# Result stores of an expert stage moved from SyncE's to ScalarE's DMA queue, tokens picked from the residual, and a ninth weight slot

## The reference

```python
def expert_block(args):
    tok_b, e = args
    xb = xpad[tok_b]
    h = jax.nn.silu(xb @ w_gate[e]) * (xb @ w_up[e])
    return h @ w_down[e]
...
out = out.reshape(rows, d) * buf_wt[:, None].astype(out.dtype)
y = jnp.zeros((t + 1, d), out.dtype).at[buf_tok].add(out)[:t]
```

## Time and profile before

| | |
|---|---|
| median of 3 runs | 1660.17 us (1656.58 to 1660.31) |
| profiled execution, its own time | 1661.11 us |
| its span | 1659.4 us |
| TensorE matmul busy | 1412.8 us (85%) |
| VectorE, ScalarE busy | 682.1 us (41%), 479.2 us (29%) |
| moved by DMA | 339.26 MB, mean 204 GB/s |
| expert stage | from about 290 to 864 us of the span |

### The profile page before, as it was taken

How to read it: one execution, slowest core, us unless ns; L and a number is a source line. 1 busy time by engine, 2 the same in 40 slices (tenths; PEclk the granted TensorE clock), 3 DMA queues, 4 the chain that set the end, 5 groups by cost and what they waited for, 6 DMA issues and landing times.

```text
span 1659.4 us, 24134 instructions
## 1 busy us (share of the span) xinstructions
PE 1412.8 (85%) x9624; PEld 1060.5 (64%) x9624; DVE 682.1 (41%) x1238; ACT 479.2 (29%) x753; POOL 40.2 (2%) x79
## 2 busy tenths in 40 slices
PE   6999997878866767796544999997999999999976
PEld 5786776645544443364223888875888888888865
DVE  4576745110111001010006656445436666656645
ACT  5452431000000000000015222233334444444432
POOL 2000000000000000000011100000000000000000
PEclk9998997989988899999876999997999999999988
DMA  8937324898999973399956555210221212121101
GB/s 351 398 127 279 127 102 203 326 406 361 380 379 423 383 327 152 139 410 395 422 224 247 214 203 182 109 52 27 102 102 51 102 52 102 52 102 52 51 1 64
DMA packets 38375, 339.26 MB, mean 204 GB/s; under 512 B 3784, under 2 KB 9800, under 8 KB 19400
## 3 DMA queue, kind: packets, MB, share of 16 engines
q1 hardware_dynamic: 30584, 302.33, 45.7%
q0 software_dynamic: 7200, 34.08, 5.8%
q10 hardware_dynamic: 432, 0.60, 0.1%
HBM read 312.62 MB, written 24.38 MB: 203 GB/s over the span
## 4 chain that ended last, share of the span: by engine, by line
PE 42%; DMA 4%; DVE 3%; ACT 2%; SPq 1%; issue 1%; POOL 0%; DVEq 0%; ACTq 0%; PEldq 0%; POOLq 0%
PE ps L285 41%; DMA y_scratch<-ar 4%; PE ps L732 1%; SPq L2087 1%; ACT ar L882 0%; DVE b_NL L1326 0%; DMA ar<-y_scratch,rt 0%; DVE ar L1318 0%; DVE hres L1796 0%; DVE hres L1789 0%; ACT b_NH L891 0%; DVE ar L1979 0%; ACT ar L1110 0%; ACT ar L1106 0%; DVE ar L1277 0%
## 5 line engine op out<-in xcount | busy, mean ns | idle before, releaser
L285 PE MATMUL ps<-ar 128*32 128x256 f32 (+5 forms) x1486 | 267.4, 397 | 53.7 <-ACT ar L1026 20.8
L285 PEld LDWEIGHTS ps<-ar 128*128 128x128 f32 (+3 forms) x1486 | 178.2, 163 | 128.5 <-issue 91.4
L285 PE MATMUL ps<-ring,ar 128*32 128x256 f32 (+1 forms) x2272 | 200.8, 411 | 47.6 <-DMA ring<-in_wts_dram 15.1
L285 PE MATMUL ps<-b_NH,b_WH 128*128 128x512 f32 x704 | 187.1, 401 | 9.5 <-ACT b_NH L891 5.1
L285 PE MATMUL ps<-b_NH,b_WL 128*128 128x512 f32 x704 | 181.0, 393 | 0.0
L1259 DVE TENSOR_TENSOR b_WL<-ring,b_WH 128x1024 fp32r<-128x1024 f32 x112 | 136.5, 1220 | 99.7 <-ACT b_WH L834 99.7
L285 PEld LDWEIGHTS ps<-ring,ar 128*32 128x32 f32 (+1 forms) x2272 | 105.4, 117 | 109.8 <-issue 61.3
L285 PE MATMUL ps<-b_NL,b_WH 128*128 128x512 f32 x704 | 173.7, 389 | 0.0
L285 PE MATMUL ps<-spare,ar 128*32 128x256 f32 (+1 forms) x1680 | 138.6, 415 | 39.4 <-ACT ar L1023 13.2
L834 ACT ACTIVATE b_WH<-ring 128x1024 fp32r<-128x1024 f32 x112 | 118.1, 1055 | 162.8 <-PE ps L285 159.8
L1689 DVE TENSOR_TENSOR ar<-ar,ps 128x128 f32<-128x128 f32 x46 | 13.1, 287 | 361.9 <-ACT ar L1020 358.6
(11 more groups left out here) (267 smaller groups left out, 1655.5 us busy)
## 6 DMA issues: line engine op xcount, KB each, us to landing
ring<-in_wts_dram SPq DMA_DIRECT2D x84, 2048.0 KB, 16.2
spare<-in_wts_dram SPq DMA_DIRECT2D x36, 2048.0 KB, 21.1
ar<-in_wts_dram SPq DMA_DIRECT2D x12, 2048.0 KB, 18.7
y_scratch<-gate POOLq DMA_DIRECT2D x15, 1024.0 KB, 25.5
ring<-in_wmod_dram SPq DMA_DIRECT2D x24, 512.0 KB, 4.6
ar<-in_wmod_dram POOLq DMA_DIRECT2D x24, 512.0 KB, 4.3
y_scratch<-ar SPq DMA_DIRECT2D x50, 128.0 KB, 2.3
hres<-in_x_dram SPq DMA_DIRECT2D x4, 512.0 KB, 6.8
```

The lines of the kernel that those rows point to most:

```text
L285: return pe.matmul(o, l, m, start=start, stop=stop, skip_group_check=True)
```

## The change

It has five parts:

- The y stores, of main, second and third blocks, are issued by ScalarE on its own queue, right behind the copy that they store. ScalarE waits for its own copy's semaphore before it issues. In the branches without a second or third block it now also waits for the landing counters `oy` and `ty` and raises them. SyncE keeps the loads; for a third block it waits for the last matmul (`t_d2`) in place of the copy.
- The picks read the residual `hres` itself; VectorE multiplies the pick matrix with the norm's factor `rs`, four more products for each set (and four in a third block).
- The first 16 KB of `ar` in each partition, where xs was, become a ninth slot, used once TensorE has transposed xs.
- The loads run nine panels ahead, so a load of expert n + 3 takes the place of the same panel of expert n.
- `mod_columns` and `mod_gate` (products for the second block's modulation) both stand behind the matmuls that rank the tokens.

```diff
-        slots = [ring[:, j, :] for j in range(RING)] + [area(4096, 4096)] + [spare[:, j, :] for j in range(3)]
+        slots = [ring[:, j, :] for j in range(RING)] + [area(4096, 4096), area(0, 4096)] + [spare[:, j, :] for j in range(3)]
...
-        for i, j in enumerate((2, 4, 0, 1, 5, 6, 7, 3)):
+        for i, j in enumerate((2, 4, 0, 1, 5, 6, 7, 8, 3)):
             settle(P_MOE + i, j)
...
-                        t = mm(ps[:, b, (k % 2) * 256:(k % 2) * 256 + 256], xs[:, p, k * 128:(k + 1) * 128],
+                        t = mm(ps[:, b, (k % 2) * 256:(k % 2) * 256 + 256], hres[:, p, k * 128:(k + 1) * 128],
                                OH[:, p, :], p == 0, p == 3)
...
+            def store(n, s):
+
+                return act.dma_start(y_d[n * CAP:(n + 1) * CAP, :].rearrange("t (q c) -> q t c", q=4), ysb[s])
...
                 copy_y(s, 5).then_inc(S["m_y"], 1)
+                act.wait_ge(S["m_y"], n + 1)
+                store(n, s).then_inc(S[f"y{s}"], 16)
...
                     copy_y(2, 7).then_inc(S["o_y"], 1)
+                    act.wait_ge(S["o_y"], n + 1)
+                    store(NE + n, 2).then_inc(S["oy"], 16)
                 with act.Else():
                     if n:
                         act.wait_ge(S["o_ht"], n)
                         act.wait_ge(S["o_y"], n)
+                        act.wait_ge(S["oy"], 16 * n)
                     act.sem_inc(S["o_ht"], 1)
                     act.sem_inc(S["o_y"], 1)
+                    act.sem_inc(S["oy"], 16)
...
+                for p in range(4):
+                    dve.wait_ge(S["m_e"], n_e[0] + 6 + p)
+                    t = dve.tensor_scalar(o[:, p, :], o[:, p, :], rs[:, p:p + 1], None, ALU.mult)
...
+            sp.wait_ge(S["turn"], 16)
+            load(P_MOE + 4)
             sp.wait_ge(S["rt_pe"], 1)
-            for i in range(P_MOE + 4, P_MOE + 7):
+            for i in range(P_MOE + 5, P_MOE + 8):
                 load(i)
...
                 with sp.If(third(n)):
-                    sp.wait_ge(S["t_y"], n + 1)
...
+                    sp.wait_ge(S["t_d2"], n + 1)
                 for m in range(3):
-                    i = P_MOE + 3 * n + m + 8
+                    i = P_MOE + 3 * n + m + 9
                     if i < P_C0:
                         load(i)
...
-                sp.wait_ge(S["m_y"], n + 1)
-                store(n, n % 2).then_inc(S[f"y{n % 2}"], 16)
```

More of the change, by code:

```diff
@@ L69, in program @@
         s_un = [ctx.enter_context(nc.semaphore(f"s_un{p}")) for p in range(4)]
-        s_slot = [ctx.enter_context(nc.semaphore(f"s_slot{j}")) for j in range(8)]
+        s_slot = [ctx.enter_context(nc.semaphore(f"s_slot{j}")) for j in range(9)]
         s_yg = [ctx.enter_context(nc.semaphore(f"s_yg{m}")) for m in range(8)]
@@ L136, in program @@
             settle(i, j)
-        for i, j in enumerate((2, 4, 0, 1, 5, 6, 7, 3)):
+        for i, j in enumerate((2, 4, 0, 1, 5, 6, 7, 8, 3)):
             settle(P_MOE + i, j)
-        for i in range(P_MOE + 8, P_C0):
-            settle(i, place[i - 8])
-        free_ring = [place[p] for p in range(P_C0 - 8, P_C0) if place[p] < RING]
+        for i in range(P_MOE + 9, P_C0):
+            settle(i, place[i - 9])
+        free_ring = [place[p] for p in range(P_C0 - 9, P_C0) if place[p] < RING]
         for i in range(P_C0, P_DIL):
@@ L517, in tensor_program @@
             t.then_inc(S["rt_pe"], 1)
+            pe.wait_ge(S["md"], 24)
+            mod_columns(acc0)
             mod_gate(acc0, (1, 6))
@@ L1026, in copy_y, with store_third @@
                 return act.activation(ysb[s], ps[:, b, 0:256], ACT.Copy)
+            def store(n, s):
+                return act.dma_start(y_d[n * CAP:(n + 1) * CAP, :].rearrange("t (q c) -> q t c", q=4), ysb[s])
+            def store_third(u):
+                r = 2 * NE * CAP + WIDE * u
+                for hf in range(2):
+                    act.dma_start(y_d[r:r + WIDE, hf * 512:(hf + 1) * 512],
+                                 ysb3[64 * hf:64 * hf + 64, :]).then_inc(S["ty"], 16)
             def third_block(u):
@@ L1039, in third_block @@
                 act.activation(ysb3, ps[:, 7, :], ACT.Copy).then_inc(S["t_y"], 1)
+                act.wait_ge(S["t_y"], u + 1)
+                store_third(u)
             act.wait_ge(S["ctl"], 1)
@@ L1724, in third_block @@
                 for p in range(4):
-                    dve.wait_ge(S["t_e"], 5 * u + 2 + p)
-                    t = dve.scalar_tensor_tensor(out=OH3[:, p, :], in0=i256[:, 0:64], scalar=rel[:, 4 + p:5 + p],
-                                                 in1=OH3[:, p, :], op0=ALU.is_equal, op1=ALU.add)
+                    dve.wait_ge(S["t_e"], 9 * u + 2 + p)
+                    dve.scalar_tensor_tensor(out=OH3[:, p, :], in0=i256[:, 0:64], scalar=rel[:, 4 + p:5 + p],
+                                             in1=OH3[:, p, :], op0=ALU.is_equal, op1=ALU.add).then_inc(S["t_e"], 1)
+                for p in range(4):
+                    dve.wait_ge(S["t_e"], 9 * u + 6 + p)
+                    t = dve.tensor_scalar(OH3[:, p, :], OH3[:, p, :], rs[:, p:p + 1], None, ALU.mult)
                 t.then_inc(S["t_oh"], 1)
@@ L2139, in sync_program @@
                         load(P_C0)
-                sp.wait_ge(S["m_y"], n + 1)
-                store(n, n % 2).then_inc(S[f"y{n % 2}"], 16)
-                with sp.If(second(n)):
-                    sp.wait_ge(S["o_y"], n + 1)
-                    if n:
-                        sp.wait_ge(S["oy"], 16 * n)
-                    store(NE + n, 2).then_inc(S["oy"], 16)
-                with sp.Else():
-                    if n:
-                        sp.wait_ge(S["oy"], 16 * n)
-                    sp.sem_inc(S["oy"], 16)
             for j in range(NOV):
```

42 lines of the change are left out of this document (13 added, 29 removed).

## The result

The changed kernel takes 1688.89 us (median of 4 runs, 1681.94 to 1692.62), the kernel before 1659.93 us in the runs beside it: a ratio of 1.0174, 95% interval 1.0137 to 1.0212, so 29 us slower. The profiled execution took 1686.87 us, 1685.1 us of it the span.

A forecast was written before the change was run, and what follows sets the result against it. Four DMA engines carrying all stores besides their weight share bound the expert stage. Terms 37.5 - 4.9 - 3.4 + 1.1 = +30 us on the median 1660.17 gave 1690 us, leaned to 1691; range 1663 to 1716.

The forecast's parts named there:

- What bounds: Expert stage: four DMA engines carry all stores besides their weight share; 510 us of work in 565 us.
- In this order the wait costs little: Expert stage before: ScalarE's 132.6 us of store waits cost little, since the four engines are working meanwhile.
- Stores on ScalarE's queue: Expert stage: queues alternate packet for packet, so a store takes 21 us while weights are queued; +37.5 us, bounds +12 to +55.
- Four dry spells: Engines idle after experts 1, 8, 15 and 22, for 6.5, 6.3, 2.6 and 5.1 us: +20.5 us.
- Issue on ScalarE: ScalarE's 46 store issues take 15 to 23 us, already in the sum; being held in issues 0, bound 0 to 10 us.
- Hole: Third blocks of experts 19 and 20: SyncE waits for the last matmul instead, one more panel in hand; -3.4 us.
- Ninth slot: Weight loads: one panel more before the loop, one less in it, on the four engines; -4.9 us.
- Factor in the pick matrix: Before the first pick: four more VectorE products, +1.1 us; the other sets lie beside TensorE's up, 0.
- Gate's matmuls later: Ahead of the picks: columns and gate end inside the wait for the pick matrix; 0, or up to +2 us.
- The store isn't held up: Rival, expert stage: small store packets go together or ahead, ScalarE's waits vanish; -26 us, 1634 us; 13%.
- Worse: Rival: ScalarE held in its issues and TensorE's lower clock at each dry spell; 1718 us at most, 1712 likely; 12%.
- the recurrence: "Latest of what it waits for" through all 32 experts; for the kernel before, expert 31's copy at 855 us, trace 858.8.

The follow-up runs named there:

- b_scalar_stores: Kernel before with only its y stores moved to ScalarE's queue, with the waits that go with them; 1689.5 us, ratio 1.0196.
- a_16_engines: Changed kernel with each y store issued by ScalarE as four transfers of 32 rows, so 16 engines can share it; 1646.99 us, ratio 0.9932.
- a_one_issue: Changed kernel, each store on ScalarE's queue as one transfer still spread over 16 engines, output not the reference's; 1625.22 us, ratio 0.9795.
- a_sync_stores: Changed kernel with the stores given back to SyncE's queue, the rest of the change kept; 1658.67 us, ratio to before 0.9989.
- a_columns_early: Changed kernel with the modulation's column matmuls back ahead of the router's ranks, as in the kernel before; 1686.11 us, ratio 1.0156.
- a_sync_16_engines: Changed kernel with stores issued by SyncE, each as four transfers spread over 16 engines; 1628.75 us, ratio 0.9809.

## Why the prediction was right, point by point

1691 us were predicted and 1688.89 measured. The mechanism was right, but that the number is so near is in part luck: the cost of the stores was sized too large, and the gain from the ninth slot, which should have been taken off it, did not come.

*What bounds.* Held: four engines. That stores spread over 16 engines gain 28 us in the kernel before, with nothing else changed, is the strongest sign of it. "In this order the wait costs little" was too kind to the kernel before: the 1.5 us of each store on the four engines were on the path all the time, and in part of the stage so was the store's place in the queue (below, at the ninth slot).

*Stores on ScalarE's queue, 32 x 0.667 = 21 us each, 42.7 a pair: +37.5.* The mechanism held: one packet for one, whatever the size. Expert 1's pair took 41.6 us from its first issue to expert 3's sigmoid. Four dry spells were named, after experts 1, 8, 15 and 22. All four came, the third around 594 us, after expert 16's first store; in the second no engine moves a packet from 471.8 to 478.8 us, 7.0 us where 6.3 were said. At the end experts 27 and 28 stand 11.6 and 16.1 us on a store (16 each were said), the last expert's last panel lands at 862.1 us (near 866) and the last copy is at 886.39 us (880 to 895). The stores' move also shortens SyncE's wait at the third blocks, which the prediction booked under the hole. The two terms together are 34.1 us in the sum, some 30 as measured (b_scalar_stores against the 1659.54 beside it); how the 4 us divide over spells and end was not followed.

*Issue on ScalarE, 0.* Held for one issue of 0.53 us per store. With four issues it costs 22 us (a_16_engines against a_one_issue), more than the bound of 10.

*Hole, -3.4.* Held: SyncE's wait falls by 8.5 us. Its waits for the third blocks, first after, then a_sync_stores, where it waits for the copy again (79.4 us in before):

```profile
SPq L2143 <- PE ps L285: 70.9, 2, 35.7
```

```profile
SPq L2129 <- ACT ar L1039: 86.3, 2, 48.6
```

In b_scalar_stores, with eight slots, they are 70.3 us. So this gain comes with the stores' move, and none of it with the ninth slot.

*Ninth slot, -4.9.* This step failed. With the slot, the factor and the matmuls' order alone (-4.9 + 1.1 = -3.8 in the sum), a_sync_stores gives 1 us. Its interval reaches to -4.3, so the time alone doesn't decide; the trace does. "One panel less" was taken as a stage that ends one panel sooner. The panels do end sooner: the last expert's last panel lands 553.0 us after the first Silu instead of 559.2. But the last copy comes 565.8 us after it, where before it was 565.6. The reason is the order in SyncE's queue. The store of expert n is issued behind the loads of its turn, which run nine panels ahead instead of eight, so it stands behind one panel more, and the copy of expert n + 2 waits for it. For experts 12 to 17 and 26 to 30 that copy comes 1.4 to 1.5 us after the last panel ahead of the store has landed, in both kernels; with nine slots this is a panel further on in the stream. What the loads gain at the start, the stores give back. Waits from 280 to 870 us, of before, then of a_sync_stores:

```profile
ACT ar L1026 <- DMA y_scratch<-ar: 132.6, 19, 15.6
...
PE ps L285 <- DMA ring<-in_wts_dram: 15.1, 3, 7.2
...
PE ps L285 <- DMA spare<-in_wts_dram: 6.8, 2, 4.1
```

```profile
ACT ar L1026 <- DMA y_scratch<-ar: 138.7, 17, 13.9
```

TensorE's waits for panels (26.4 us in 6 with one at `ar`) are gone in a_sync_stores, ScalarE's waits for stores are not. In the changed kernel the stores have left that queue, and still the slot gives nothing to be seen: from first Silu to last copy it takes 595.6 us, b_scalar_stores with eight slots 594.5. Why not there stays open.

*Factor in the pick matrix, +1.1.* Held as a step: the four products take 1.13 us (from 270.26 us in after), and the picks begin 27.9 us after TensorE starts the router's transposes, 26.6 before.

*Gate's matmuls later, 0.* Right in the time, wrong in the trace. It is the columns' matmuls, moved along with them, that fill the pause ahead of the picks, which so run 2.6 us shorter than before, at a higher clock. That gain was not foreseen; by a_columns_early nothing of it is left in the time.

*Rivals.* "The store isn't held up" fell at the first rows. Its size was no fancy, though: 1634 us was its forecast, and the versions in which stores really aren't held up long stand at 1625 to 1632. "Worse" had two parts: ScalarE was never held in an issue (1.11 us at most), and the lower clock in the spells is seen (0.50 to 0.59 over them), but the measured time leaves no room for it on top of the sum.

*Where the experiments' forecasts failed.* a_16_engines was forecast 39 us too low at its upper end. a_one_issue takes the four issues out and gains 22 us. The other 17 stay open. One thing in the trace is not in the recurrence: TensorE's pauses at L652, of which the earlier trace rows show one. They are 42 to 46 us in the versions with spread stores, but they are no product of the spreading: before has 30.6 us in 11, a_sync_stores 45.3 in 17. Nor would they all come back if they went, for the DMA engines are full beside them, here in a_sync_16_engines:

```profile
300.00:590.00 290.00, 230.07 (x2854) 145.89 (x2846) 35.73 (x96) 23.89 (x79) 0.00 (x0) 0.96 1.00 415
```

What the pauses are was not tested. They follow experts without second block, where TensorE jumps over a part of its program, and ahead of each of the 17 in a_16_engines and the 11 in before one 16 KB packet of the instruction queue q8 moves (it has some 75 in the stage); it starts 3.4 to 3.9 us ahead of the end of every pause over 2.5 us. That fits a wait for instructions, and no run here takes it away to see.

## What to carry to other kernels

Ask of each small transfer how many engines it takes and how many of its rows stand on one of them: beside a bulk load, a store on a queue of its own is as slow as rows per engine times the time of one bulk row. On the queue of the bulk load it stands behind all that was issued before it, so loading further ahead moves it back. Spreading it (here the outermost dimension 32 or 128 instead of 4) was worth 28 to 30 us, and moving it to another queue without spreading cost as much. And where a wait is only for keeping count, keep it on an engine that nobody waits for: its place was 13 us here.

## What was not expected of the hardware

- On a single queue too, a store's rows cost the bulk load beside them: 46 stores of 128 KB, 6 MB of 193, held the stage up by 28 us as long as all of them went to four of sixteen engines.
- The time of an issue on ScalarE depends on the form of the transfer: 0.33 us for one of 128 KB whose outermost dimension is 128, 0.53 us with an outermost dimension of 4, 0.44 us (median) for each of four of 32 KB.
- The fastest form (1625.22 us) needs a scratch in which a token's quarters lie in separate rows; a gather that reads it so was not tried.
